# Where the sample scores and the dense group lie among forty index-score chunks

## The reference, cut to what matters

```python
s = einsum('bqhd,bsd->bqhs', q_i, k_i) * IDX_DIM ** -0.5
score = einsum('bqhs,bqh->bqs', relu(s), w_i * IDX_HEADS ** -0.5)
score = where(key_pos <= t_pos, score, -inf)
_, idx = top_k(score, topk)
```

## Time and profile before

| | |
|---|---|
| median of 3 runs | 2051.84 us (2047.83 to 2054.05) |
| profiled execution, its own time | 2051.95 us |
| its span | 2050.3 us |
| TensorE busy (matmul) | 1979.9 us, 97% |
| VectorE busy | 1036.7 us, 51% |
| ScalarE busy | 627.2 us, 31% |
| the score stage | 66.5 to 101.1 us |

### The profile page before, as it was taken

The page is one execution under the profiler, slowest core; times in us unless marked ns, Lnnn a source line. Parts: engine busy times, 40 slices in busy tenths (PEclk is TensorE's granted clock), DMA queues, the critical chain, the costliest instruction groups (busy, mean ns, idle before and its releaser), DMA issues.

```text
span 2050.3 us, 31168 instructions
## 1 busy us (share of the span) xinstructions
PE 1979.9 (97%) x12165; PEld 1809.4 (88%) x12165; DVE 1036.7 (51%) x2226; ACT 627.2 (31%) x1125; POOL 313.6 (15%) x327
## 2 busy tenths in 40 slices
PE   6899999999999999999799999999999999999996
PEld 6599999999999888888699878999999999999995
DVE  5699994445444423666654335424432443344335
ACT  5533212322333364555443213212111121121112
POOL 3343223332222231011024200000000000000001
PEclk9999999999999999999899999999999999999998
DMA  5132332222221254344654221011101110111002
GB/s 163 37 89 84 115 111 88 84 81 71 69 68 48 80 181 145 116 168 158 224 167 136 77 101 62 1 62 62 62 1 62 62 62 1 62 62 56 7 21 95
DMA packets 144099, 174.44 MB, mean 85 GB/s; under 512 B 9560, under 2 KB 120958, under 8 KB 143454
## 3 DMA queue, kind: packets, MB, share of 16 engines
q1 hardware_dynamic: 136638, 148.89, 22.2%
q0 software_dynamic: 7328, 23.67, 3.3%
HBM read 127.83 MB, written 44.40 MB: 84 GB/s over the span
## 4 chain that ended last, share of the span: by engine, by line
PE 89%; DVE 5%; ACT 2%; issue 1%; DMA 1%; SPq 0%; POOL 0%; DVEq 0%; ACTq 0%; POOLq 0%
PE ring L937 25%; PE ring L939 25%; PE ring L938 25%; PE ring L1097 3%; PE ring L932 3%; PE lgt L1087 2%; PE ring L1257 1%; DMA od_whole<-dsa_outputs 1%; PE ring L1264 1%; PE ring L1043 1%; DVE arena L2477 1%; PE lgt L1333 0%; PE ring L1260 0%; DVE arena L1974 0%; DVE arena L2418 0%
## 5 line engine op out<-in xcount | busy, mean ns | idle before, releaser
L937 PE MATMUL ring<-n_hi,piece_hi 128*128 128x352 f32 (+1 forms) x1312 | 435.6, 332 | 2.6 <-ACT arena L1400 1.7
L939 PE MATMUL ring<-n_hi,piece_lo 128*128 128x352 f32 (+1 forms) x1312 | 424.0, 323 | 0.0
L938 PE MATMUL ring<-n_lo,piece_hi 128*128 128x352 f32 (+1 forms) x1312 | 423.1, 322 | 0.0
L1400 ACT ACTIVATE arena<-ring 128x352 f32<-128x352 f32 (+7 forms) x367 | 152.5, 439 | 421.7 <-PE ring L939 301.4
L937 PEld LDWEIGHTS ring<-n_hi,piece_hi 128*128 128x128 f32 (+1 forms) x1312 | 247.3, 188 | 10.7 <-issue 6.9
L938 PEld LDWEIGHTS ring<-n_lo,piece_hi 128*128 128x128 f32 (+1 forms) x1312 | 248.0, 189 | 0.4
L939 PEld LDWEIGHTS ring<-n_hi,piece_lo 128*128 128x128 f32 (+1 forms) x1312 | 246.9, 188 | 0.3
L1988 DVE TENSOR_SCALAR_CACHE_REDUCE arena<-arena 128x384 uint8<-128x384 f32 (+6 forms) x224 | 190.6, 874 | 1.4 <-DVE arena L1988 0.2
L2496 POOL TENSOR_TENSOR piece_lo<-piece_whole,piece_hi 128x1024 fp32r<-128x1024 f32 (+2 forms) x48 | 109.1, 2272 | 517.0 <-ACT piece_hi L1413 516.9
L937 PE MATMUL ring<-h_hi,gate_hi 128*128 128x352 f32 x528 | 170.5, 323 | 0.7 <-DVE act_whole L2427 0.7
L937 PE MATMUL ring<-h_hi,up_hi 128*128 128x352 f32 x528 | 170.3, 323 | 0.0
(11 more groups left out here) (309 smaller groups left out, 3634.5 us busy)
## 6 DMA issues: line engine op xcount, KB each, us to landing
piece_whole<-w_in SPq DMA_DIRECT2D x54, 512.0 KB, 3.8
projected_rows<-arena SPq DMA_DIRECT2D x44, 528.0 KB, 2.7
arena<-projected_rows SPq DMA_DIRECT2D x12, 1056.0 KB, 6.2
gate_whole<-w_ffn_gate SPq DMA_DIRECT2D x11, 1024.0 KB, 7.2
up_whole<-w_ffn_up SPq DMA_DIRECT2D x11, 1024.0 KB, 9.3
down_whole<-w_ffn_down SPq DMA_DIRECT2D x11, 1024.0 KB, 5.0
arena<-projected_rows SPq DMA_DIRECT2D x16, 528.0 KB, 3.6
arena<-x_prompt SPq DMA_DIRECT2D x16, 512.0 KB, 6.7
```

The source lines that it names most:

```text
L937: pe.matmul(out, lhi, rhi, start=first, stop=False)
L938: pe.matmul(out, lhi, rlo, start=False, stop=False)
L939: return pe.matmul(out, llo, rhi, start=False, stop=last)
L1400: evacuates(act.activation(dst, src, ACT.Copy, scale=scale), *key)
```

## The change

The four parts of the dense group move from before chunks 10, 12, 14 and 16 to before chunks 2, 6, 10 and 14. The sample products move from before chunks 4 and 8 to before chunks 22 and 27, and their relus on ScalarE from before chunks 8 and 12 to before chunks 24 and 29. On VectorE the weights and multiplications move from before chunk 15 to before chunk 31. The sums on TensorE move from before chunk 24 to before chunk 34, in the ring's numbering too, and the rows' copy on VectorE from before chunk 27 to before chunk 37.

```diff
         def score_groups(n):
-            return range(2 * (n - 10) // 2, 2 * (n - 10) // 2 + 2) if 10 <= n < 18 and n % 2 == 0 else []
+            return {2: range(0, 2), 6: range(2, 4), 10: range(4, 6), 14: range(6, 8)}.get(n, [])
+
+        SI_AT = {HALF + 2: 0, HALF + 7: 1}
+        SS_AT = HALF + 14
...
         for n, k in enumerate(SCC):
-            if n == HALF + 4:
+            if n == SS_AT:
                 plan("ss")
...
                 if score_groups(n):
                     dense_part(2, 1, score_groups(n)[0], score_groups(n)[-1] + 1)
-                if n in (4, 8):
-                    sample_scores(n // 4 - 1)
+                if n in SI_AT:
+                    sample_scores(SI_AT[n])
...
-                if n == HALF + 4:
+                if n == SS_AT:
                     sample_sums()
...
-                if n in (8, 12):
-                    g = n // 4 - 2
+                if n - 2 in SI_AT:
+                    g = SI_AT[n - 2]
                     wait_full(act, "si", g)
...
-                if n == 15:
+                if n == HALF + 11:
                     sample_weights()
                     weigh_sample()
-                if n == HALF + 7:
+                if n == SS_AT + 3:
                     sample_rows()
```

## The result

| | before | after |
|---|---|---|
| median, 7 runs each | 2048.67 us (2047.54 to 2054.05) | 2056.01 us (2051.88 to 2058.34) |
| ratio | | 1.0031, 95% interval 1.0019 to 1.0043 |
| profiled execution, span | 2050.3 us | 2051.5 us |
| score stage on TensorE, first chunk to last | 34.58 us | 39.33 us |
| first chunk to VectorE's first work of the attention | 269.17 us | 274.37 us |

The change makes the kernel slower, by 0.31%: 6.4 us of 2048.67, between 3.9 and 8.8. The two profiled spans lie only 1.2 us apart; the profiled execution of before was one of its slower ones (2051.95 against a median of 2048.67), that of after one of its faster ones (2053.19), so the spans can't be compared; the stage can.

A forecast was written before the change was run, and what follows sets the result against it. TensorE, busy 97% of the span, was taken to bound the kernel. The profiled 2051.95 us plus 0.55 for order and 1.45 for clock made 2053.95; with the runs' median 0.11 lower, 2053.8 us, range 2048.5 to 2057.5.

The forecast's parts named there:

- TensorE bounds, and only its end of the stage counts: Score stage: TensorE is busy 97% of the span, so only when it leaves the stage affects the time.
- VectorE could slip by 7.3 us "for nothing": VectorE's end of the stage may come up to 7.3 us later free, its next work after the search idling 7.33 us.
- First half 2.7 us shorter: Chunks 0 to 19: chunk 20 starts on TensorE at 81.45 us, 2.7 us earlier than 84.17.
- 2.8 us earlier either way: First half: the whole dense group comes 2.8 us earlier with or without spreading its parts, so spreading alone gives little.
- Group 0's products leave a hole of 1.3 us at chunk 22: Second half: sample products before chunk 22 find TensorE without lead, so VectorE stands still about 1.3 us.
- Group 1's cost 0.1: Second half: sample products before chunk 27 cost 0; their relu before chunk 29 adds 0.1 us.
- Sample weights 1.31 us on VectorE, with nothing for contention: Before chunk 31: 1.31 us of VectorE's time, none hidden; 0 taken for GpSimd contention, worst case +0.7.
- 0.55 us for the order at full clock: End of the score stage: TensorE leaves 0.55 us later than before, the first half's gain being given back in the second.
- Sums late by 0.5 us for chunk 34, hole of 1.25 at chunk 37: Chunk 34 reaches VectorE 0.5 us late; the ring wait moves from chunk 27 to 37 at the same price, 0 added.
- The clock, one slow stretch of 3.2 us, 1.45 us: Behind TensorE's 2.8 us wait before chunk 37: 3.2 us at half clock, all on the path, costing 1.45 us.
- rival D: Thin work from about 90 to 108 us keeps TensorE at 1.2 GHz into the first dense groups: 2058.7 us, chance 0.05.
- E, the change does not do what it says: Rival: first half stays TensorE's, chunk 20 comes no earlier, while the second half grows: 2055 us, chance 0.07.

The follow-up runs named there:

- the kernel with fillers: The change plus 26 idle products on TensorE, 14 before the sample sums and 12 before chunk 37, against the kernel before: ratio 1.0003.

## Why the prediction was right or wrong

The time lay in the range (2056.01 in 2048.5 to 2057.5), and slower than before was the forecast's direction; the size was not right. I had put the shift at 2.0 us; it was 6.4. That the absolute number came within 2.2 us is luck, two errors that cancel: I counted from runs at 2051.8 to 2052, which is 3.2 us too high (four more runs of before moved its median to 2048.67), and my shift was 4.4 us too small. Against the 0.3%, 6.15 us, that I had named as what a measurement tells from no change, I had given "same" 0.90 and "slower" 0.06, and slower is what came.

- *TensorE bounds, and only its end of the stage counts*: right. VectorE's wait at the attention grew from 7.33 to 12.70 us, by 5.37, and TensorE lost 5.20. That VectorE could slip by 7.3 us "for nothing" does not follow from the row, as said above; here its last score came 3.4 us later in the stage (40.94 us after chunk 0 instead of 37.52), and nobody waited for it.
- *First half 2.7 us shorter*: 17.63 - 15.07 = 2.56. Right. That spreading the dense parts is worth little by itself is shown by the kernel that did only this. The reason that I gave for it, "2.8 us earlier either way", is wrong: without the spread chunk 20 came only 1.23 us earlier (16.40).
- *Group 0's products leave a hole of 1.3 us at chunk 22*: 1.27. Right. *Group 1's cost 0.1*: the hole at chunk 28 is 1.00 where it was 1.26, so they cost nothing.
- *Sample weights 1.31 us on VectorE, with nothing for contention*: 91.96 to about 93.37, 1.41; the two multiplications took 0.71 instead of 0.62. Nearly right, but not for the reason weighed: GpSimd's subtraction was over at 92.51 (88.66 for 3.85 us), before the multiplications began at 92.74, so whether it would stretch them this trace does not show. Only GpSimd's short selections (from 92.46) ran beside them.
- *0.55 us for the order at full clock*: 1.1, in the kernel with fillers. VectorE's second half grew by what I had added up, 3.0 us (from 83.25 to 104.58 is 21.3, against 18.3). The 0.6 us missed are 0.3 of the first half (VectorE's chunk 20 came 2.57 us earlier, not 2.85) and 0.3 of TensorE's lead at the end (104.58 - 102.32 = 2.3, not 2.6).
- *Sums late by 0.5 us for chunk 34, hole of 1.25 at chunk 37*: 1.95 and 2.85. At full clock, in the kernel with fillers, they are 0.41 and 1.91. So the first term was right at its clock. The second was too small by 0.66 at any clock: I had priced it by the hole at chunk 27, which is 128 wide, and chunk 37 is 512 wide; the 1.92 that I used two lines on for TensorE's end was its price. That the sum for the second half came out right all the same is luck: other terms were too large, group 1's by 0.36. The rest, 1.5 and 0.9 us, is the half clock.
- *The clock, one slow stretch of 3.2 us, 1.45 us*: this is the step that failed, and the largest part of the error. The mechanism was named, and the place (the thin work between the two waits) too, but the slow stretch lasted 17.1 us. I had taken its length from the two rows of before, each slow for 3.4 us, as if the length were a property of the fall. What the runs show in its place is that it goes with what follows: with the wait before chunk 37 taken away or filled, the stretch that began at the like place lasted 6.8 us (one trace each), and the time fell by 7.4 and 4.9 us. It is no rule for one trace: with only the sample work moved there were two such waits and two stretches of 6.8 us with 3.4 between them, not one. And I had started it at chunk 37, not before the sums. What came is rival D, to which I gave 0.05: thin work from about 90 us keeps the clock down into the dense groups. I had held against it that "in the rows the clock came back after 3.1 and 3.8 us"; but neither of those stretches had a wait of 2 us behind its start.
- The price of D by its own rule: 17.1 us slow at 0.45 is 7.7, less 1.45 for each slow stretch of before that lay in dense work (one), plus 0.55: 6.8. To the attention the traces show 5.2, since part of the slow time lay in TensorE's waits; the timed runs 6.4.
- *E, the change does not do what it says*: false; it was the first half that did exactly what it should.

The shown part of the cause: the moved sample work (only that edit: 1.0040; only the other: 1.0001), and the clock that it brings down (idle products in its waits: 1.0003; granted clock over the timed executions 0.987, against 0.989 to 0.990 before). What stays open: when the clock falls within the thin work, how a filler keeps it up, and why executions differ. The single execution profiled of each kernel shows between 0 and 17 us slow from 60 to 130 us, with other falls elsewhere (near 20, 735, 770, 782, 982, 1018 and 1161 us) that come and go from kernel to kernel; timed runs of the change alone lie 6.5 us apart. So the split of the 6.4 us into 1.1 of order and the rest of clock rests on two traces; the ratios say only that nearly all of it goes with idle products.

## What to carry to other kernels

Where the engine that bounds has a stretch of thin work, a wait in it costs its own length and also what the clock takes afterwards, from the dense work behind it: here the kernel without one wait of 2.05 us was some 7.4 us faster, 3 either way. So do not move small serial chains (weights, sums, their copies) to where that engine is already paced by another, and do not let a small result take a turn in a ring that the pace-setting stream uses (in the change its own bank took the ratio from 1.0031 to 0.9995; in before, where a dense group did not follow so soon, only to 0.9994, which is not told from 1); if a hole can't be avoided, put the next full-size work into it, cut into parts (0.9979 and 0.9983). When a forecast has a "slow stretch" in it, its length depends on what will run in it, waits too, and can't be taken over from another stretch; and one trace does not tell whether it comes at all.

## What the runs showed of the hardware

- Slow stretches of TensorE were 3.4, 6.8 or 17.1 us long here, and a stage can hold several: 3.4 + 6.8 + 6.8 us in the kernel with only the sample work moved.
- The clock fell to 1.2 GHz at 98.9 us, behind 14 us (84 to 98) in which TensorE's records cover 12.43 us and no hole is over 0.56 us; busy time in the records does not tell whether the clock will hold. The trace of before has the same at 108.3 us: slow, behind a stretch from 101.12 that the records cover without a gap.
- A wait of 3.12 us before the same chunk was followed by 3.4 us at 1.2 GHz in one kernel's execution and by full clock in another's, with the same instructions around it. A fall 25.4 us after chunk 0 came in one execution and not in another that had run the same instructions at the same distances up to there.
- 26 products with no use, over 4 us of TensorE's time at full clock, made the change about 5.7 us faster.
